# MoBA's position bias from a skewed table: VectorE adds it while it takes the maxima, in place of flip-matrix products on TensorE

## The chip, the cores and the metric

The kernel runs on one core of one Trainium2 chip. The metric is the device time of one execution in microseconds. Lower is better.

## What is computed

Two transformer programs run one after the other (a macaron block of depth 2 with a time mixer, MoBA attention and cross attention, then a second block of depth 2). The change lies in MoBA attention in the first one. There are 256 positions, 8 heads of 64 columns and one block of 256 keys, so the block-sparse attention comes down to causal attention with a position bias:

```python
q = to_heads(q) * (Dh ** -0.5)
...
bias_own = rel_bias[:, rel_bucket(q_pos[:, None] - own_pos[None, :])]
s_own = jnp.einsum('bhqd,bhkd->bhqk', q_c, k_own).astype(f32) + bias_own.astype(f32)[None]
s_own = jnp.where(own_pos[None, :] <= q_pos[:, None], s_own, -jnp.inf)
...
probs = jax.nn.softmax(logits, axis=-1).astype(v.dtype)
```

The bias depends on the head and on the distance of query and key alone. The mask can be written into it: keys ahead of the query have a bias of -1e30.

## The kernel before

Everything of the first program lives in SBUF; weights stream through a ring of six 1 MB slots. Each engine has its own program, written out by hand, and waits on counting semaphores. `nc.sync` loads the weights: a slot is loaded as soon as TensorE has used the tile in it. ScalarE and VectorE split each weight tile into a high and a low part before TensorE multiplies (`col_high`, `col_low`).

A layer goes: feed-forward 1, mixer projection (13 column tiles), MoBA (`moba(l)` on TensorE), the time mixer's solver and recurrence, keys and values of the cross attention, and so on. MoBA starts when the last projection tile (the values `mv`) is copied out of PSUM, and the solver starts when MoBA's last output is copied out.

**The bias.** After feed-forward 1 of layer 0 TensorE makes one row of 512 biases per head (products with a one-hot matrix of distances), and VectorE copies them to `bias_rows`, 8 partitions that lie inside `mv`. GpSimd stores them (16 KB) in DRAM and reads them back with a step of one element per partition (`modulation_program`, L1187 and L1190): `hank[p, h, t] = row_h[p + t]`. This table is in the reverse order of partitions, and a product with the flip matrix `cst["flip"]` turns it round on TensorE. The table is made once and used in both layers. ScalarE waits for the store to be done before it writes to `mv`.

**MoBA.** A head's scores fill one PSUM bank with two query tiles: queries 128 to 255 against 256 keys, and queries 0 to 127 against 128 keys. Four banks rotate. The engines go over the heads like this:

- TensorE (`moba`): in step h `scores(h)`, then `turn(h - 2)` (three 128x128 transposes of the probabilities, L808), then `out(h - 3)` (products with the values, L817 and L818). `scores(h)` has four products: two with the flip matrix (L793, L795), which put the bias into the bank, and two of queries and keys (L797, L799) that add to it.
- VectorE (`softmax`): `maxima(h)` (two maxima over the bank, L1759, and a negation, L1763), then `weights(h - 1)` (reciprocal of the sums, L1768, and two multiplications, L1771), then for every second head the copy of an output pair (L1781). After head 3 it also has `col_low(l, KV0)`, the low part of the first key-value tile (128x2048, L1572).
- ScalarE (`softmax`): `exponential(h)` from PSUM into `prob` with the sum read out (L1351), then `turned(h - 2)`, which copies the turned block to SBUF (L1361).

`prob` has four buffers, so with the exponential of head h ScalarE waits until head h - 4 was turned. TensorE waits with the scores of head h until ScalarE has read the bank of h - 4. The same helper `softmax` serves the cross attention, without bias.

Of the kernel before, what the change touches and what calls it, by code (L numbers as in the profile page):

```python
# [19 lines left out]
ALU = mybir.AluOpType  # L20
# [4 lines left out]
P = 128  # L25
T = 256
# [77 lines left out]
def constants():  # L104

    i = np.arange(P)
    r, c = i[:, None], i[None, :]
    f = lambda m: m.astype(np.float32)
    j, t = i[:, None] % CH, np.arange(CH)[None, :]
    blocks = {  # L110
        "ident": f(r == c),
        "ones": np.ones((P, P), np.float32),
        "head_ones": f(r // HD == c // HD),
        "flip": f(r + c == P - 1),
        "eye": f(j == t),
        "upper": f(j < t),
        "upper_incl": f(j <= t),
        "upper_sub": f((j < t) & (j // SUB == t // SUB)),
        "lower_sub": f((j > t) & (j // SUB == t // SUB)),
        "lower_off": f((j > t) & (j // SUB != t // SUB)),  # L120
    }

    blocks["carry"] = np.tile(f(np.arange(T) % CH != 0), (P, 1))
    return blocks
# [122 lines left out]
def program(nc, a, out):  # L247

    with ExitStack() as ctx:
# [7 lines left out]
        for name, c in constants().items():  # L257
# [12 lines left out]
        store["v_loaded"] = [Signal(ctx, nc, f"v_loaded{s}") for s in range(RING2)]  # L270
        scratch = {"bias": nc.dram_tensor("bias_scratch", (NH, 2 * T), F32).ap(),
                   "mod": nc.dram_tensor("mod_scratch", (DEPTH, P, 2, MODS * P), F32).ap()}
# [10 lines left out]
def build_first(nc, ctx, a, scratch, store):  # L283
# [4 lines left out]
    def sb(name, shape):  # L288
        return ctx.enter_context(nc.sbuf_tensor(name, shape, F32))
# [10 lines left out]
    with ExitStack() as under:  # L300
# [11 lines left out]
        part("under_mem", [P, KD, T])  # L312
        part("under_hank", [P, NH, T])
        g_low = part("g_low", [P, KD, T])
# [20 lines left out]
    mem_sb = sb("mem_sb", [P, KD, T])  # L335
    hank = sb("hank", [P, NH, T])
    mix_buf = sb("mix_buf", [P, RAW + 4 * T])
# [272 lines left out]
    def tensor_program(pe):  # L610
# [175 lines left out]
        def moba(l):  # L786
            def scores(h):
                pair, hb, bank = h // 2, (h % 2) * HD, ps[SCORE_BANKS[h % 4]]
                if h >= 4:
                    pe.wait_ge(*sm_act.at(l, 2 * (h - 3)))  # L790
                hi = slice(hb, hb + HD)

                mm(bank[:, 0:T], cst["flip"], hank[:, h, :], start=True, stop=False,  # L793
                   skip_group_check=True)
                mm(bank[:, T:T + P], cst["flip"], hank[:, h, P:T], start=False, stop=False,  # L795
                   skip_group_check=True)
                mm(bank[:, 0:T], mq[hi, pair, P:T], mk[hi, pair, :], start=False, stop=False,  # L797
                   skip_group_check=True)
                mm(bank[:, T:T + P], mq[hi, pair, 0:P], mk[hi, pair, 0:P], start=False, stop=True,  # L799
                   skip_group_check=True).then_inc(*sc_done.up())  # L800

# [20 lines left out]
            pe.wait_ge(*mix_evac.at(l, MIX_TILES - 1))  # L822
            if l == 0:
                pe.wait_ge(bias_stored.sem, 32)
            for h in range(NH + 3):
# [332 lines left out]
    def modulation_program(pool):  # L1158
# [19 lines left out]
        for n in range(DEPTH * MOD_CHUNKS):  # L1178
# [6 lines left out]
            if n == FFN_STEPS // 2 - 1:  # L1185
                pool.wait_ge(*mem_placed.at(0, 5))
                pool.dma_start(scratch["bias"], bias_rows).then_inc(bias_stored.sem, 16)  # L1187
                pool.wait_ge(bias_stored.sem, 16)
                src = scratch["bias"]
                pool.dma_start(hank[:, :, :], bass.AP(src.tensor, 0, [[1, P], [2 * T, NH], [1, T]])  # L1190
                               ).then_inc(bias_stored.sem, 16)
# [4 lines left out]
    def scalar_program(act):  # L1196
# [144 lines left out]

        def softmax(l, base, scale, widths, banks):

            def exponential(h):
                e, g, bank = h % 4, base + h, ps[banks[h % 4]]
                act.wait_ge(*sm_max.at(l, 3 * (g + 1)))
                if h >= 4:
                    act.wait_ge(*pt_done.at(l, g - 3))
                at = 0
                for t, w in enumerate(widths):  # L1350
                    go(prob[:, e, at:at + w], bank[:, at:at + w], ACT.Exp, bias=smx[:, e, t:t + 1],  # L1351
                       scale=scale, accum_out=ssum[:, e, t:t + 1]).then_inc(*sm_act.up())
                    at += w
# [42 lines left out]
        for l in range(DEPTH):  # L1396
# [72 lines left out]
            col_high(l, KV0)  # L1469
            exponential, turned = softmax(l, 0, 1.0, (T, P), SCORE_BANKS)  # L1470
            for h in range(NH + 2):
# [59 lines left out]
    def vector_program(dve):  # L1531
# [220 lines left out]

        def softmax(l, base, scale, widths, banks):
            def maxima(h):
                e, g = h % 4, base + h
                dve.wait_ge(*sc_done.at(l, g + 1))
                at = 0
                for t, w in enumerate(widths):
                    v.tensor_reduce(smx[:, e, t:t + 1], ps[banks[e]][:, at:at + w], AX_X, ALU.max  # L1759
                                    ).then_inc(*sm_max.up())  # L1760
                    at += w
# [145 lines left out]
        for l in range(DEPTH):  # L1907
# [61 lines left out]
            step(l, v.memset(state[:, :, :], 0.0), seq_step)  # L1969
            maxima, weights = softmax(l, 0, 1.0, (T, P), SCORE_BANKS)  # L1970
            evac = moba_out(l)
# [1603 lines left out]
```

## Time and profile before

| | us |
|---|---|
| median of 3 runs | 2476.46 |
| lowest and highest | 2475.26, 2477.57 |
| span of the profiled execution | 2475.7 |

The profiled execution's own time is not given apart from these runs; its span lies 0.8 us under their median and inside what they spread over. The page gives the busy time of each engine; the trace gives single instructions, merged where alike follow one another. A merged row has the start of the first, the length of all, and in brackets the idle time before it with what ended it.

### The profile page before, as it was taken

The page shows a single profiled execution, that of the slowest core. Times are in us where ns is not written, and L with a number is a line of the kernel's source. Part 1 is how long each engine was busy: PE and PEld are TensorE (multiplying, and loading weights), DVE is VectorE, ACT ScalarE, POOL GpSimd, SP SyncE. Part 2 cuts the span into 40 slices and gives each one's busy share as a digit, 9 for nine tenths or more (in the row PEclk, how much of TensorE's full clock was granted, in tenths as well). Part 3 has the DMA queues.
Part 4 walks back from the last instruction along what each step waited for, and adds up shares of the span by engine and source line. Part 5 has one row for each costly group of instructions (what it writes and reads, how often), then busy time and mean ns, then how long its engine had stood idle before and what let it go on. Part 6 is the DMA issues. An engine that isn't in the chain of part 4 may idle for free. (4 is left out here: it accounts for less than half of the span.)

```text
span 2475.7 us, 41693 instructions
## 1 busy us (share of the span) xinstructions
PE 2411.7 (97%) x17447; PEld 2055.0 (83%) x17447; DVE 1606.0 (65%) x2242; ACT 1033.3 (42%) x1365; POOL 99.2 (4%) x179
## 2 busy tenths in 40 slices
PE   7999999999999999999999999999999999998999
PEld 7999989999999999899999854464888887647999
DVE  6887756778888887657798632671744442474555
ACT  5445534454554455335454321661422222263333
POOL 2010000001101100000001000000000000000000
PEclk9999999999999999999999999999999999999999
DMA  8776503647777775116467742102532331212452
GB/s 283 251 271 216 168 3 120 205 145 267 252 254 239 272 244 160 46 54 213 162 229 255 272 155 68 52 2 71 167 102 90 98 102 52 81 56 69 162 195 69
DMA packets 270807, 381.97 MB, mean 154 GB/s; under 512 B 9593, under 2 KB 235209, under 8 KB 268994
## 3 DMA queue, kind: packets, MB, share of 16 engines
q1 hardware_dynamic: 251628, 314.47, 38.7%
q0 software_dynamic: 18128, 64.20, 7.2%
q8 instruction: 114, 1.87, 0.3%
q10 hardware_dynamic: 902, 1.15, 0.2%
q14 instruction: 35, 0.29, 0.0%
HBM read 366.13 MB, written 13.65 MB: 153 GB/s over the span
## 5 line engine op out<-in xcount | busy, mean ns | idle before, releaser
L704 PE MATMUL ps<-span 128*128 128x512 f32 x1280 | 453.9, 399 | 2.3 <-issue 1.2
L635 PE MATMUL ps<-span,w_low 128*128 128x256 f32 x1440 | 408.0, 283 | 0.0
L706 PE MATMUL ps<-span,w_low 128*128 128x256 f32 x1280 | 359.5, 281 | 0.0
L633 PE MATMUL ps<-span 128*128 128x256 f32 x1216 | 348.6, 287 | 8.2 <-DVE span L1585 5.2
L1603 DVE TENSOR_TENSOR w_low<-ring,span 128x2048 fp32r<-128x2048 f32 x131 | 299.8, 2288 | 82.3 <-ACT span L1267 82.3
L1267 ACT ACTIVATE span<-ring 128x2048 fp32r<-128x2048 f32 x131 | 250.6, 1915 | 135.5 <-DMA ring<-in_ffn_w_in 112.8
L704 PEld LDWEIGHTS ps<-span 128*128 128x128 f32 x1280 | 240.6, 188 | 60.3 <-issue 1.3
L635 PEld LDWEIGHTS ps<-span,w_low 128*128 128x128 f32 x1440 | 277.0, 192 | 0.0
L634 PE MATMUL ps<-span 128*128 128x256 f32 x864 | 245.3, 284 | 0.0
L633 PEld LDWEIGHTS ps<-span 128*128 128x128 f32 x1216 | 233.8, 192 | 12.4 <-DVE w_low L1603 5.4
L706 PEld LDWEIGHTS ps<-span,w_low 128*128 128x128 f32 x1280 | 241.9, 189 | 0.0
L1624 DVE SCALAR_TENSOR_TENSOR mod_acc<-wmod,cond,mod_acc 128x512 f32<-128x512 f32 x336 | 232.3, 748 | 0.4 <-DMA wmod<-in_w_mod 0.4
L634 PEld LDWEIGHTS ps<-span 128*128 128x128 f32 x864 | 166.5, 193 | 0.2
L1572 DVE TENSOR_TENSOR w_low<-ring,span 128x2048 fp32r<-128x2048 f32 x50 | 114.2, 2291 | 51.1 <-ACT span L1210 50.6
L3229 DVE TENSOR_TENSOR w_low<-ring,w_high 128x2048 fp32r<-128x2048 f32 x32 | 73.3, 2292 | 71.8 <-ACT w_high L2958 71.8
L2931 ACT ACTIVATE w_high<-ring 128x2048 fp32r<-128x2048 f32 x32 | 61.2, 1913 | 126.3 <-PE ps L2611 126.3
L1277 ACT ACTIVATE prob<-ps 128x512 f32<-128x512 f32 x80 | 47.7, 596 | 157.0 <-PE ps L706 156.8
L1166 POOL DMA_DIRECT2D wmod<-in_w_mod x96 | 70.6, 735 | 1028.3 <-DVE mod_acc L1624 806.9
L1210 ACT ACTIVATE span<-ring 128x2048 fp32r<-128x2048 f32 x50 | 94.8, 1908 | 21.9 <-PE ps L635 20.5
L2958 ACT ACTIVATE w_high<-ring 128x2048 fp32r<-128x2048 f32 x32 | 61.2, 1916 | 100.4 <-PE ps L2551 100.4
L2705 PE MATMUL ps<-h_sb,ring 128*128 128x512 f32 (+1 forms) x256 | 96.8, 540 | 4.8 <-ACT h_sb L2919 4.6
L2609 PE MATMUL ps<-act_halves,w_high 128*128 128x512 f32 x256 | 100.6, 393 | 0.0
(487 smaller groups left out, 5337.3 us busy)
## 6 DMA issues: line engine op xcount, KB each, us to landing
ring<-in_ffn_w_in SPq DMA_DIRECT2D x88, 1024.0 KB, 8.9
ring<-in_w_mlp SPq DMA_DIRECT2D x64, 1024.0 KB, 5.3
wmod<-in_w_mod POOLq DMA_DIRECT2D x96, 512.0 KB, 6.8
ring<-in_ffn_w_out SPq DMA_DIRECT2D x44, 1024.0 KB, 5.2
ring<-in_w_mix_in SPq DMA_DIRECT2D x26, 1024.0 KB, 5.5
ring<-in_xattn_w_kv SPq DMA_DIRECT2D x16, 1024.0 KB, 5.4
mod_scratch<-mod_acc POOLq DMA_DIRECT2D x24, 512.0 KB, 6.2
ring<-mod_scratch SPq DMA_DIRECT2D x12, 1024.0 KB, 4.9
```

The source lines that it names most:

```text
L633: mm(dst, w_hi, x_hi, start=start, stop=False, **more)
L634: mm(dst, w_hi, x_lo, start=False, stop=False, **more)
L635: return mm(dst, w_lo, x_hi, start=False, stop=stop, **more)
L704: mm(ps[bank + m].rearrange("p (w t) -> p w t", w=2), hi[:, k, cols], span[:, :, k, :], start=(k == 0), stop=False, skip_group_check=True)
L706: last = mm(ps[bank + m][:, 0:T], lo[:, k, cols], h_high[:, k, :], start=False, stop=(k == KD - 1), skip_group_check=True)
L1210: go(w_high[COLUMN_HIGHS[c]], slot(n), ACT.Copy).then_inc(*column_high.up())
L1267: go(w_high[buffer], ring[:, tiles.slot(r, b), :], ACT.Copy).then_inc(w_high_ready.sem, 1)
L1572: v.tensor_tensor(w_low[:, n % RING, :], slot(n), w_high[COLUMN_HIGHS[c]], ALU.subtract).then_inc(*column_low.up())
L1603: v.tensor_tensor(w_low[:, slot, :], ring[:, slot, :], w_high[buffer], ALU.subtract).then_inc(w_low_ready.sem, 1)
L1624: v.scalar_tensor_tensor(mod_acc[:, c, :], w, col, mod_acc[:, c, :], ALU.mult, ALU.add).then_inc(mod_step.sem, 1)
L2609: mm(out, w_hi, x_hi, start=start, stop=False)
L2705: last = mm(ps[bank + m][:, c], wt[:, k, m * P:(m + 1) * P], h[:, k, c], start=(k == 0), stop=(k == KD - 1))
```

## The change

The row of biases is stored 128 times per head (2 MB), once for each partition, and read back with a step of one element less than a row, so that each partition gets the row shifted by one more: `toep[p, h, t] = row_h[127 - p + t]`. This is the table in its right order, so the flip matrix goes. VectorE adds it: in `maxima(h)` one `tensor_tensor_reduce` per query tile reads scores from PSUM and the table from SBUF, writes the sum to `prob` and the maximum to `smx`. The exponentials then read and write `prob`. The wait for the turn of head h - 4 moves from ScalarE to VectorE; TensorE waits with scores(h) for the maxima of h - 4 in place of its exponentials; and the wait for the table in layer 0 moves from TensorE to VectorE.

```diff
-        "flip": f(r + c == P - 1),
...
-        scratch = {"bias": nc.dram_tensor("bias_scratch", (NH, 2 * T), F32).ap(),
+        scratch = {"bias": nc.dram_tensor("bias_scratch", (NH, P, 2 * T), F32).ap(),
...
-    hank = sb("hank", [P, NH, T])
+    toep = sb("toep", [P, NH, T])
...
                 if h >= 4:
-                    pe.wait_ge(*sm_act.at(l, 2 * (h - 3)))
+                    pe.wait_ge(*sm_max.at(l, 3 * (h - 4) + 2))
                 hi = slice(hb, hb + HD)
-
-                mm(bank[:, 0:T], cst["flip"], hank[:, h, :], start=True, stop=False,
-                   skip_group_check=True)
-                mm(bank[:, T:T + P], cst["flip"], hank[:, h, P:T], start=False, stop=False,
-                   skip_group_check=True)
-                mm(bank[:, 0:T], mq[hi, pair, P:T], mk[hi, pair, :], start=False, stop=False,
-                   skip_group_check=True)
-                mm(bank[:, T:T + P], mq[hi, pair, 0:P], mk[hi, pair, 0:P], start=False, stop=True,
-                   skip_group_check=True).then_inc(*sc_done.up())
+                mm(bank[:, 0:T], mq[hi, pair, P:T], mk[hi, pair, :], start=True, stop=True)
+                mm(bank[:, T:T + P], mq[hi, pair, 0:P], mk[hi, pair, 0:P], start=True, stop=True
+                   ).then_inc(*sc_done.up())
...
-            if l == 0:
-                pe.wait_ge(bias_stored.sem, 32)
...
-                pool.dma_start(scratch["bias"], bias_rows).then_inc(bias_stored.sem, 16)
+                pool.dma_start(scratch["bias"], bias_rows.rearrange("h (o t) -> h o t", o=1).to_broadcast(
+                    [NH, P, 2 * T])).then_inc(bias_stored.sem, 16)
...
-                pool.dma_start(hank[:, :, :], bass.AP(src.tensor, 0, [[1, P], [2 * T, NH], [1, T]])
+                pool.dma_start(toep[:, :, :], bass.AP(src.tensor, P - 1, [[2 * T - 1, P], [P * 2 * T, NH], [1, T]])
...
-                e, g, bank = h % 4, base + h, ps[banks[h % 4]]
+                e, g = h % 4, base + h
+                bank = prob[:, e, :] if biased else ps[banks[h % 4]]
                 act.wait_ge(*sm_max.at(l, 3 * (g + 1)))
-                if h >= 4:
-                    act.wait_ge(*pt_done.at(l, g - 3))
...
                 dve.wait_ge(*sc_done.at(l, g + 1))
+                if biases and h >= 4:
+                    dve.wait_ge(*pt_done.at(l, g - 3))
                 at = 0
                 for t, w in enumerate(widths):
-                    v.tensor_reduce(smx[:, e, t:t + 1], ps[banks[e]][:, at:at + w], AX_X, ALU.max
-                                    ).then_inc(*sm_max.up())
+                    if biases:
+                        v.tensor_tensor_reduce(prob[:, e, at:at + w], ps[banks[e]][:, at:at + w], biases(h, t), 1.0,
+                                               -3.0e38, ALU.add, ALU.max, smx[:, e, t:t + 1]).then_inc(*sm_max.up())
+                    else:
+                        v.tensor_reduce(smx[:, e, t:t + 1], ps[banks[e]][:, at:at + w], AX_X, ALU.max
+                                        ).then_inc(*sm_max.up())
...
-            maxima, weights = softmax(l, 0, 1.0, (T, P), SCORE_BANKS)
+            if l == 0:
+                dve.wait_ge(bias_stored.sem, 32)
+            maxima, weights = softmax(l, 0, 1.0, (T, P), SCORE_BANKS, lambda h, t: toep[:, h, t * P:T])
```

TensorE's list in MoBA, one steady step, before (`sm_act` counts exponentials, `sm_norm` weights, `pt_ready` copies of turned blocks):

```order
L793 MATMUL ps<-hank,consts_sb 128x256 [waits sm_act]
L795 MATMUL ps<-hank,consts_sb 128x128
L797 MATMUL ps<-mk,mq 128x256
L799 MATMUL ps<-mk,mq 128x128
L808 MATMUL ps<-consts_sb,prob 128x128 [waits pt_ready,sm_norm]
L808 MATMUL ps<-consts_sb,prob 128x128 x2
L817 MATMUL ps<-probT,mv 64x256 [waits pt_ready]
L818 MATMUL ps<-probT,mv 64x128
```

The same step now (`sm_max` counts maxima):

```order
L791 MATMUL ps<-mk,mq 128x256 [waits sm_max]
L792 MATMUL ps<-mk,mq 128x128
L801 MATMUL ps<-consts_sb,prob 128x128 [waits pt_ready,sm_norm]
L801 MATMUL ps<-consts_sb,prob 128x128 x2
L810 MATMUL ps<-probT,mv 64x256 [waits pt_ready]
L811 MATMUL ps<-probT,mv 64x128
```

The two bias products are gone, and the wait of the step stands at the scores.

VectorE's list in MoBA, the step of head 5, before (`sc_done` counts scores, `av_out` output copies):

```order
L1759 TENSOR_REDUCE smx<-ps 128x1 [waits sc_done,av_out]
L1759 TENSOR_REDUCE smx<-ps 128x1
L1763 TENSOR_SCALAR smx<-smx 128x2 [waits sm_max]
L1768 RECIPROCAL ssum<-ssum 128x2 [waits sm_act]
L1771 TENSOR_SCALAR prob<-prob,ssum 128x256 [waits sm_norm]
L1771 TENSOR_SCALAR prob<-prob,ssum 128x128
```

The same step now (`pt_done` counts turns):

```order
L1753 ISA prob,smx<-ps,toep 128x256 [waits pt_done,sc_done,av_out]
L1753 ISA smx 128x1
L1753 ISA prob,smx<-ps,toep 128x128
L1753 ISA smx 128x1
L1760 TENSOR_SCALAR smx<-smx 128x2 [waits sm_max]
L1765 RECIPROCAL ssum<-ssum 128x2 [waits sm_act]
L1768 TENSOR_SCALAR prob<-prob,ssum 128x256 [waits sm_norm]
L1768 TENSOR_SCALAR prob<-prob,ssum 128x128
```

Each maximum became an addition with a running maximum and a separate readout of it (the rows with `smx` alone), and the wait for the turn stands at the head of the step.

## Rows read from the trace of the kernel before

**Rows 1.** The page, its span and part 1: busy time of each engine.
```profile
span 2475.7 us, 41693 instructions
...
PE 2411.7 (97%) x17447; PEld 2055.0 (83%) x17447; DVE 1606.0 (65%) x2242; ACT 1033.3 (42%) x1365; POOL 99.2 (4%) x179
```

**Rows 2.** Windows, MoBA in both layers: length, busy per engine, granted clock, DMA share, GB/s.
```profile
302.98:327.75 24.77, 23.60 (x121) 16.95 (x121) 14.97 (x53) 12.25 (x41) 0.00 (x0) 1.00 0.13 43
1001.31:1026.08 24.77, 23.60 (x120) 16.95 (x121) 14.98 (x53) 12.21 (x41) 0.00 (x0) 1.00 0.14 43
```

**Rows 3.** Timeline, TensorE, one steady head: start, us, engine, line, operation [idle before].
```profile
317.24 0.70 PE L793 MATMUL ps<-hank,consts_sb 128*128 128x256 f32 x2
...
318.09 0.70 PE L797 MATMUL ps<-mk,mq 64*128 64x256 f32 x2
...
318.93 0.55 PE L808 MATMUL ps<-consts_sb,prob 128*128 128x128 f32 x3
...
319.41 0.65 PE L817 MATMUL ps<-probT,mv 128*64 128x256 f32 x2
...
320.20 0.70 PE L793 MATMUL ps<-hank,consts_sb 128*128 128x256 f32 x2
```

**Rows 4.** Timeline, all engines, the first head of layer 0.
```profile
303.80 0.70 PE L797 MATMUL ps<-mk,mq 64*128 64x256 f32 x2
...
304.83 0.62 DVE L1759 TENSOR_REDUCE smx<-ps 128x1 f32<-128x256 f32 x2 [4.26 <-PE ps L799]
...
305.48 0.17 DVE L1763 TENSOR_SCALAR smx<-smx 128x2 f32<-128x2 f32 x1
...
305.69 0.47 ACT L1351 ACTIVATE prob<-ps,smx 128x256 f32<-128x256 f32 x1 [1.00 <-DVE smx L1763]
...
306.06 0.19 ACT L1351 ACTIVATION_READ_ACCUMULATOR prob<-ps,smx 128x1 f32 x1
306.15 0.36 ACT L1351 ACTIVATE prob<-ps,smx 128x128 f32<-128x128 f32 x1
...
306.40 0.20 ACT L1351 ACTIVATION_READ_ACCUMULATOR prob<-ps,smx 128x1 f32 x1
...
307.19 0.16 DVE L1768 RECIPROCAL ssum<-ssum 128x2 f32<-128x2 f32 x1
...
307.38 0.55 DVE L1771 TENSOR_SCALAR prob<-prob,ssum 128x256 f32<-128x256 f32 x2
```

**Rows 5.** Groups by form, whole span: busy us, mean ns of one, idle before.
```profile
L1572 DVE TENSOR_TENSOR w_low<-ring,span 128x2048 fp32r<-128x2048 f32 x50 | 114.2, 2291 | 51.1 <-ACT span L1210 50.6
...
L1759 DVE TENSOR_REDUCE smx<-ps 128x1 f32<-128x256 f32 x32 | 12.8, 422 | 23.3 <-PE ps L799 18.1 <-PE ps L1028 5.2
...
L1814 DVE TENSOR_TENSOR sc<-ps,sc 128x256 f32<-128x256 f32 x24 | 10.2, 425 | 17.7 <-PE ps L873 17.5
...
L1361 ACT ACTIVATE probT<-ps 128x384 f32<-128x384 f32 x16 | 7.7, 489 | 2.0 <-PE ps L808 2.0
```

**Rows 6.** Groups by form: VectorE's multiply-add of two SBUF tensors and a scalar column.
```profile
L1624 DVE SCALAR_TENSOR_TENSOR mod_acc<-wmod,cond,mod_acc 128x512 f32<-128x512 f32 x336 | 232.3, 748 | 0.4 <-DMA wmod<-in_w_mod 0.4
```

**Rows 7.** Groups by form: a ScalarE pass of 128x512 from PSUM and from SBUF.
```profile
L1277 ACT ACTIVATE prob<-ps 128x512 f32<-128x512 f32 x80 | 47.7, 596 | 157.0 <-PE ps L706 156.8
...
L1282 ACT ACTIVATE prob<-prob 128x512 f32<-128x512 f32 x40 | 24.7, 618 | 11.4 <-DVE prob L1636 11.2
```

**Rows 8.** Timeline, layer 0: the first turn and the last output copy.
```profile
308.04 0.55 PE L808 MATMUL ps<-consts_sb,prob 128*128 128x128 f32 x3
...
327.18 0.42 DVE L1781 COPY cat<-ps 128x256 f32<-128x256 f32 x1 [1.57 <-PE ps L818]
```

**Rows 9.** GpSimd's store, the read of the table (DMA view), ScalarE's first write to `mv`.
```profile
217.74 0.55 POOL L1187 DMA_DIRECT2D bias_scratch<-mv  x1 [21.39 <-DVE mv L1924]
...
hank<-bias_scratch POOLq DMA_DIRECT2D x1, 1024.0 KB, 6.0
...
294.84 0.60 ACT L1334 ACTIVATE mv<-ps 128x512 f32<-128x512 f32 x1 [3.41 <-PE ps L764]
```

More of the change, by code:

```diff
@@ L312, in build_first @@
         part("under_mem", [P, KD, T])
-        part("under_hank", [P, NH, T])
+        part("under_toep", [P, NH, T])
         g_low = part("g_low", [P, KD, T])
@@ L1340, in cross_part, with softmax @@
                ).then_inc(*cross_high.up())
-        def softmax(l, base, scale, widths, banks):
+        def softmax(l, base, scale, widths, banks, biased=False):
             def exponential(h):
-                e, g, bank = h % 4, base + h, ps[banks[h % 4]]
+                e, g = h % 4, base + h
+                bank = prob[:, e, :] if biased else ps[banks[h % 4]]
                 act.wait_ge(*sm_max.at(l, 3 * (g + 1)))
-                if h >= 4:
-                    act.wait_ge(*pt_done.at(l, g - 3))
                 at = 0
@@ L1469, in scalar_program @@
             col_high(l, KV0)
-            exponential, turned = softmax(l, 0, 1.0, (T, P), SCORE_BANKS)
+            exponential, turned = softmax(l, 0, 1.0, (T, P), SCORE_BANKS, True)
             for h in range(NH + 2):
@@ L1751, in shift, with softmax @@
                                                b[:, m, 1:T + 1], ALU.mult, ALU.add), mixed)
-        def softmax(l, base, scale, widths, banks):
+        def softmax(l, base, scale, widths, banks, biases=None):
             def maxima(h):
```

## The prediction

> **What bounds the kernel now.** I read the page first: TensorE is busy 97% of a span of 2475.7 us, VectorE 65%, ScalarE 42% [rows 1]. So time is won only where TensorE's own list gets shorter and nothing else steps in. The change touches one stage that runs once per layer, MoBA's attention, so next I read the windows of that stage: 24.77 us in each of two layers, with TensorE busy for 23.60 of it, VectorE for 14.97, ScalarE for 12.2, at a granted clock of 1.00 [rows 2]. The timeline of one head in the steady part shows TensorE going round without a gap: bias products and scores from 317.24, of which the bias products last to 318.09 (0.85 us), the scores to 318.93 (0.84), the turning of probabilities to 319.41 (0.48), the products with the values to 320.20 (0.79) [rows 3]. A head costs 2.97 us, and VectorE and ScalarE idle inside it. That is the limit that the change attacks, 0.85 of each 2.97 us.
>
> **What goes from TensorE.** Two products per head, 0.85 us, 8 heads, 2 layers: 13.6 us of TensorE's time. This would be the gain only if the others kept up, and 2.12 us per head is about what their chain needs, so I worked that chain out.
>
> **The prices on the other engines.** From the first head of layer 0 [rows 4]: the maximum sees a finished score product 0.18 us after its end (303.80 + 0.85, then 304.83); the two maxima take 0.62, the negation follows 0.03 later and takes 0.17; ScalarE's exponentials start 0.04 after it and end at 306.60, 0.91 later. The weights (reciprocal and two multiplications) take from 307.19 to 307.93. ScalarE's copy of the turned block takes 0.49, the copy of an output pair on VectorE 0.42 [rows 5, 8]. Between such steps 0.03 to 0.06 us pass, 0.10 to 0.15 after a product. The large subtraction for the first key-value tile that sits in VectorE's list after head 3 takes 2.29 [rows 5].
>
> **What VectorE gets.** In place of two maxima it issues four instructions per head: an addition with running maximum over 256 columns, a readout of the maximum, the same for 128 columns, another readout. Call the length of this block M; before it is 0.62. No such instruction is in the trace. The main part is nearest to the addition of a PSUM and an SBUF tensor of 128x256, 425 ns, which equals the maximum's 422 ns [rows 5], so the main parts alone leave M at 0.62. For the readout the nearest row is ScalarE's: 0.19 us long, but the next exponential starts 0.09 after it (306.06, 306.15), because it overlaps the end of its main part [rows 4]. With that overlap M = 0.62 + 0.09 + 0.09 = 0.80. With no overlap at all it is 0.42 + 0.20 + 0.28 + 0.20 = 1.10. Bounds: 0.62 if readouts are hidden; above, 1.5, if the main part also runs at half rate (256 and 128 columns more at the 1.1 ns per column of the 2291 ns subtraction over 2048 [rows 5], 0.42 us). I take M = 0.90, nearer the row with the overlap, with 0.10 for an instruction form that nothing here has timed.
>
> The microarchitecture reference of the Trainium skill (Vector Engine (DVE) Microarchitecture Reference, section "Points that are easy to get wrong") says that an accumulating two-source instruction with both fp32 sources in SBUF runs at half rate. By it alone M would be about 1.3 to 1.5. Here one source is PSUM; and the two-SBUF-source form without accumulation takes 748 ns for 512 columns [rows 6], far from half rate, but no row has the accumulating form.
>
> **What ScalarE gets.** The exponentials read SBUF in place of PSUM. The same 128x512 pass over SBUF took 618 ns, over PSUM 596 [rows 7]: 0.022 more each, 0.05 per head. Its wait for the earlier turn goes (to VectorE, below). Setting this to 0 changes the sum by 0.3 us.
>
> **The waits that move.** VectorE now waits before head h's block, for h of 4 and up, until TensorE has turned head h-4. Queued behind that wait are all its later weights and output copies, and TensorE waits for those; but the turn of h-4 lies two rounds back in TensorE's list, so I cost it at nothing. TensorE's wait before scores(h) is now on the maxima of h-4, also long past: nothing. What replaces them is the plain supply of probabilities.
>
> **The replay.** I went through the 8 heads list by list: an instruction starts at the later of its engine's previous end and its releaser. With the costs of before it puts the last output copy at 327.5 against 327.18 in the trace, a fair check (0.2 of it is one turn that overlaps the next bias product). With the bias products out and M = 0.90:
> - Scores(0) start at 302.98 as before [rows 4], maxima(0) at 304.01 in place of 304.83. VectorE then does maxima(1) at 305.02 and must wait for the exponentials of head 0: weights(0) at 306.14, turn(0) at 306.94. Before it was at 308.04 [rows 8]. TensorE has been idle 1.4 us, so of 2.55 us taken from its list 1.10 is gained.
> - Turn(1) 308.64; turn(2) 311.00. VectorE's 2.2 us subtraction lies from 310.23 to 312.43. Maxima(4) follow it, weights(3) at 313.44, turn(3) at 314.24, after a wait of 1.1 (before, TensorE did not notice the subtraction).
> - After that a round of two heads is closed through ScalarE: scores and their 0.18 (1.03), block and negation (0.90 + 0.24), exponentials (0.85), copy (0.54), values (0.79) = 4.35, or 2.18 per head, against 2.12 that TensorE needs. The turns come at 316.60, 318.72, 320.71 and 322.22.
> - The last output copy starts at 324.43, 3.1 us before the replay of the old kernel; in the trace it starts at 327.18 and the next stage at 327.75 [rows 2, 8].
>
> So 3.1 us per layer, 6.2 in all, less than half of the 13.6. The sum by other M, from the same replay, both layers: 0.62 gives 8.6 less; 0.80, 7.2; 1.00, 5.0; 1.10, 3.6; 1.20, 2.2; 1.36, nothing; 1.50, 2.1 more; 1.70, 5.3 more. What follows the stage waits for its last copy on TensorE, so the gain is passed on; the weight loads there are released by TensorE's use, and move with it.
>
> **The table.** The row of biases is now written to DRAM 128 times, 2 MB in place of 16 KB, once, from 217.74, and read back skewed. The 1 MB read took 6.0 us [rows 9], so 2 MB are 12, and I allow twice that because it leaves from few partitions. So it lands by 242, and the table by 250. ScalarE needs the row's place at 294.84 [rows 9], VectorE the table at 304. So I cost it at nothing: ScalarE's own work covers it with 50 us to spare, and past that it costs the delay itself. The weight loads that share the DMA engines with it are issued six tiles ahead.
>
> **Sum.** The profiled span is 2475.7, the median of the three runs 2476.46 (0.8 above; the fastest is 2475.26). 2476.46 - 6.2 = 2470.3 us.
>
> **Rivals.** What a measurement here can tell from no change is about 0.2%, 5 us.
> - *Readouts do not overlap* (M 1.0 to 1.3). For: a readout needs the last column's result; against: ScalarE's overlaps. 2471.5 to 2475.9, at M = 1.1 2472.9. 0.27.
> - *Readouts are hidden* (M to 0.75): 2468, for: VectorE's small instructions overlap by 0.08 each. 0.06.
> - *The block runs at half rate*, as the skill's rule above would have it if PSUM does not help: M = 1.5, VectorE becomes the bound, 2478.6. Against it, the 748 ns. 0.10.
> - *Slower:* this kind of instruction has a fixed cost of its own that nothing hides, since every one waits for or feeds the next. Place: VectorE's block between score and exponential. Four per head; from M = 1.36 (0.14 each above the 0.80 sum) the kernel loses, from 1.68 (0.22 each) by over 5 us; at M = 1.7, 2481.8. For: no instruction of this form has a row. Against: all others on VectorE keep to one line of length over columns. 0.06.
> - *The table is late*, because 128 copies leave from only 8 partitions: it would need over three times the 24 us. 2480 or far more. 0.02.
> - *The change does not do what it says*, as the gain is taken back by a later wait: within 2 us of 2476.5. 0.03.
>
> **Numbers.** The forecast (M 0.75 to 1.0, 2468.9 to 2471.5) has 0.46. Faster by over 0.2% is this and the hidden readouts, less a little at the edge: 0.50. Within 0.2%: 0.27 + 0.10 + 0.03 + that edge = 0.42. Slower: 0.08. The range goes from 2467.8 (M = 0.62) to 2478.0, which leaves out the two slow cases and half of the half-rate one.
>
> **What would show it.** In the stage's window: TensorE's turns 2.1 to 2.2 us apart in place of 2.97, now with idle time released by VectorE's weights or ScalarE's copy; turn(0) at 1.1 us earlier; stage 21.7 us long in both layers. The new instructions near 425 and 280 ns and readouts that add 0.1. I am wrong if the main part is over 0.5 us, if the readouts stand beside it in full, if turn(3) comes later than 315, or if ScalarE's conversion near 294.8 waits for the stored row.

## The result and the profile after

| | time, median us | runs | profiled span |
|---|---|---|---|
| before | 2477.02 | 4 (2475.26 to 2479.95) | 2475.7 |
| changed | 2499.02 | 4 (2498.95 to 2500.17) | 2496.9 |

The changed kernel is slower: its ratio to the kernel before is 1.0093, with a 95% interval of 1.0079 to 1.0108. I had forecast 2470.3. That is 22 us in the runs and 21.2 us in the profiled span, and the span can be taken apart.

The page of the changed kernel: its span, the busy time of each engine, and the granted clock over 40 slices.

```profile
span 2496.9 us, 41593 instructions
...
PE 2418.5 (97%) x17383; PEld 2055.2 (82%) x17383; DVE 1606.6 (64%) x2274; ACT 1033.5 (41%) x1365; POOL 99.5 (4%) x179
...
PEclk9999989999999999899999999999999999999999
```

Against [rows 1], TensorE executes 64 instructions fewer and is busy for 6.8 us *longer* (2418.5 against 2411.7). An engine with less work and more busy time points to its clock. The slices of 62 us are too coarse to show where. The windows below are finer: MoBA's stage in both layers, then pieces of the stage in layer 0, then two stretches ahead of it. Columns as in [rows 2].

```profile
316.31:344.39 28.08, 25.16 (x88) 15.90 (x89) 15.33 (x69) 12.65 (x41) 0.00 (x0) 0.64 0.12 38
1018.71:1046.79 28.08, 25.17 (x88) 15.63 (x89) 15.33 (x69) 12.57 (x41) 0.00 (x0) 0.64 0.12 38
316.31:320.10 3.79, 1.55 (x13) 1.30 (x13) 2.30 (x14) 3.49 (x9) 0.00 (x0) 1.00 0.85 262
322.00:341.00 19.00, 19.00 (x55) 11.58 (x56) 10.90 (x46) 7.33 (x27) 0.00 (x0) 0.50 0.00 1
341.00:344.39 3.39, 2.71 (x15) 1.64 (x14) 0.85 (x2) 0.64 (x2) 0.00 (x0) 0.95 0.00 0
262.00:266.00 4.00, 0.00 (x0) 0.00 (x0) 0.00 (x0) 1.50 (x1) 1.02 (x2) 0.61 0.94 307
266.00:270.00 4.00, 1.04 (x5) 1.07 (x6) 3.41 (x4) 3.51 (x5) 0.00 (x0) 0.50 1.03 338
```

Two things are to be seen. The stage takes 28.08 us in place of 24.77, in both layers, and for most of it the granted clock is 0.50, the level of 1.2 GHz, where [rows 2] show 1.00, that of 2.4 GHz. And the stage of layer 0 begins at 316.31 in place of 302.98: 13.3 us were lost before it, and from 262 to 266 TensorE does nothing at all. So 13.3 + 3.3 + 3.3 = 19.9 of the 21.2 us have a place. The other 1.3 lie in the rest of the program, which the change does not touch; nothing here shows what they are.

**The first place.** The DMA view of 215 to 275 us (what is written, from what, queue, count, size, median us from issue to landing), then the time to landing of the loads that were issued from 215 to 270:

```profile
ring<-in_w_mix_in SPq DMA_DIRECT2D x6, 1024.0 KB, 26.2
bias_scratch<-mv POOLq DMA_DIRECT2D x1, 2048.0 KB, 45.0
toep<-bias_scratch POOLq DMA_DIRECT2D x1, 1024.0 KB, 9.3
...
DMA to landing us min/median/max: 13.7/26.2/41.1
```

The timelines of SyncE (an issue of a load), ScalarE and TensorE, with the idle time before an instruction in brackets:

```profile
223.40 0.37 SPq L551 DMA_DIRECT2D ring<-in_w_mix_in  x1
...
264.50 1.91 ACT L1202 ACTIVATE span<-ring 128x2048 fp32r<-128x2048 f32 x1 [15.23 <-DMA ring<-in_w_mix_in]
...
268.96 0.55 PE L632 MATMUL ps<-span 128*128 128x256 f32 x1 [10.06 <-DVE w_low L1563]
```

The store of the table takes 45.0 us, from 218.16 to 263.2; the one of 16 KB before took 1.8. The median of 26.2 us for the 1 MB loads of mixer weights mixes two kinds. The three that were issued while the store ran, at 223.40, 229.99 and 236.90, took 41.1, 37.4 and 36.4 us, and the first of them landed only at 264.5, behind the end of the store. In the kernel before, the loads issued at 222.97, 229.55 and 236.47 took 7.3, 5.3 and 5.3. The issue at 236.90 also took 24.55 us itself in place of 0.37, so the loads behind it left late. GpSimd's own wait for the store (44.2 us) costs nothing. The wait that does is ScalarE's for the load of 223.40: ScalarE comes for it at 249.27, 25.9 us after its issue, and waits 15.23. The wait passes through VectorE's `w_low` to TensorE, which stands idle for 10.06. Inside that idle time the granted clock falls to 0.50, and it is back at 1.00 in the window of 274 to 276. So 10.1 of the 13.3 us are idle time, and of the 3.3 behind it the slow clock is a part. The table itself came in time: it landed near 273, and ScalarE, which needs the row's place in `mv`, came to it only at 308.13.

**The second place.** The timeline of the changed kernel, TensorE and VectorE, start of the stage and two later steps (start, us, [idle before]):

```profile
316.31 0.71 PE L791 MATMUL ps<-mk,mq 64*128 64x256 f32 x4 [0.78 <-ACT mv L1326]
...
317.04 0.59 PE L791 MATMUL ps<-mk,mq 64*128 64x256 f32 x2
...
317.39 0.42 DVE L1753 CUSTOM_DVE_ANT_0 prob<-ps,toep 128x256 f32<-128x256 f32 x1 [3.52 <-PE ps L792]
...
317.74 0.08 DVE L1753 DVE_READ_ACCUMULATOR2_ANT smx<- 128x1 f32 x1
317.74 0.28 DVE L1753 CUSTOM_DVE_ANT_0 prob<-ps,toep 128x128 f32<-128x128 f32 x1
317.95 0.08 DVE L1753 DVE_READ_ACCUMULATOR2_ANT smx<- 128x1 f32 x1
318.07 0.17 DVE L1760 TENSOR_SCALAR smx<-smx 128x2 f32<-128x2 f32 x1
...
320.10 0.55 PE L801 MATMUL ps<-consts_sb,prob 128*128 128x128 f32 x3 [2.24 <-DVE prob L1768]
...
324.19 1.22 PE L791 MATMUL ps<-mk,mq 64*128 64x256 f32 x2
...
328.07 1.22 PE L791 MATMUL ps<-mk,mq 64*128 64x256 f32 x2
```

The scores of heads 0 to 2 are done at 317.86. Then TensorE waits 2.24 us for the first probabilities. The granted clock is 1.00 up to 320 and 0.50 from 321 on. From then on the same score product takes 1.22 us in place of 0.70 [rows 3], and one head takes 3.88 us (324.19 to 328.07).

VectorE's new block runs from 317.39 to 318.03, so the prediction's M, the length of this block, is 0.64. The main parts take 0.42 and 0.28. The first readout (0.08) begins at the same time as the second main part, the last one ends the block.

So two theories stand for the 22 us. The **store theory**: the store of 2 MB costs 12 to 13 us, through the weights. The **clock theory**: TensorE's idle time ahead of `turn(0)` (the first turn, which waits for the first probabilities) drops its clock, and that costs the stage more than the change takes from it. The main rival of the second: VectorE is the bound of the shorter stage (a block too long, a wait moved wrong), and the clock follows from a TensorE that waits.

### The profile page after: what moved, and what is told of

Same layout as the page of the kernel before. It is cut to its first block and busy times, and to the rows that moved or that the text cites. A ratio compares the mean times of both kernels' runs of the same rounds, so it can differ in the third digit from the quotient of the medians.

```text
span 2496.9 us, 41593 instructions
## 1 busy us (share of the span) xinstructions
PE 2418.5 (97%) x17383; PEld 2055.2 (82%) x17383; DVE 1606.6 (64%) x2274; ACT 1033.5 (41%) x1365; POOL 99.5 (4%) x179
## 5 line engine op out<-in xcount | busy, mean ns | idle before, releaser
L632 PEld LDWEIGHTS ps<-span 128*128 128x128 f32 x1216 | 234.8, 193 | 22.3 <-issue 12.4
```

Source lines behind the costliest of these rows:

```text
L632: mm(dst, w_hi, x_hi, start=start, stop=False, **more)
```

## Experiments

**1. The table is made without the wide store.** The row goes to DRAM once, is copied there 128-fold from DRAM to DRAM, and then read as in the change.

```
-        scratch = {"bias": nc.dram_tensor("bias_scratch", (NH, P, 2 * T), F32).ap(),
+        scratch = {"row": nc.dram_tensor("bias_row", (NH, 2 * T), F32).ap(),
+                   "bias": nc.dram_tensor("bias_scratch", (NH, P, 2 * T), F32).ap(),
...
-                pool.dma_start(scratch["bias"], bias_rows.rearrange("h (o t) -> h o t", o=1).to_broadcast(
+                pool.dma_start(scratch["row"], bias_rows).then_inc(bias_stored.sem, 16)
+                pool.wait_ge(bias_stored.sem, 16)
+                pool.dma_start(scratch["bias"], scratch["row"].rearrange("h (o t) -> h o t", o=1).to_broadcast(
                     [NH, P, 2 * T])).then_inc(bias_stored.sem, 16)
-                pool.wait_ge(bias_stored.sem, 16)
+                pool.wait_ge(bias_stored.sem, 32)
...
-                dve.wait_ge(bias_stored.sem, 32)
+                dve.wait_ge(bias_stored.sem, 48)
```

> The change, but the 2 MB of shifted biases are made otherwise: the 16 KB of rows are stored once from SBUF, a DRAM to DRAM transfer copies them 128 times, and the table is read back as before. Theory: the store that leaves from 8 partitions held the DMA engines for 45 us and starved the mixer weights, 13.3 us ahead of MoBA in layer 0; from DRAM the 2 MB take under 15 us, the stall goes, MoBA starts near 303 us, and the time is 2499.0 - 13.3 = 2485 to 2486 us, with the granted clock still near 0.64 over MoBA in both layers. Rival: 2 MB more of traffic at that place is the trouble however they are made; then most of the stall stays and the time is above 2493.

Measured: 2486.83 us in the median of 6 runs; ratio to before 1.0039 (1.0026 to 1.0051), 12 us less than the changed kernel (12.4 by the profiled spans, 2484.5 against 2496.9). Its DMA view of the same stretch, and its windows of the stage:

```profile
ring<-in_w_mix_in SPq DMA_DIRECT2D x7, 1024.0 KB, 5.5
bias_scratch<-bias_row POOLq DMA_DIRECT2D x1, 2048.0 KB, 16.1
```

```profile
303.16:331.31 28.15, 25.23 (x88) 15.82 (x89) 15.32 (x69) 12.64 (x41) 0.00 (x0) 0.64 0.13 38
1006.45:1034.55 28.10, 25.21 (x89) 15.85 (x89) 15.32 (x69) 12.64 (x41) 0.00 (x0) 0.64 0.13 38
```

The same 2 MB take 16.1 us. The loads of weights take 5.5 in the median; the three issued at 223 to 237, during the copy or just behind it, take 14.1, 10.4 and 9.3, which is slower than before but inside the 25.9 us that ScalarE leaves them. ScalarE has no wait for weights, and the stage begins at 303.16, close to the 302.98 of before. It is still 28.1 us long at a clock of 0.64. The two losses are apart.

**2. The wide store alone, in the kernel before.** Everything stays as it was, flip products too, but the row is stored 128 times, and `hank` is read from the first copy of each head.

```
-        scratch = {"bias": nc.dram_tensor("bias_scratch", (NH, 2 * T), F32).ap(),
+        scratch = {"bias": nc.dram_tensor("bias_scratch", (NH, P, 2 * T), F32).ap(),
...
-                pool.dma_start(scratch["bias"], bias_rows).then_inc(bias_stored.sem, 16)
+                pool.dma_start(scratch["bias"], bias_rows.rearrange("h (o t) -> h o t", o=1).to_broadcast(
+                    [NH, P, 2 * T])).then_inc(bias_stored.sem, 16)
...
-                pool.dma_start(hank[:, :, :], bass.AP(src.tensor, 0, [[1, P], [2 * T, NH], [1, T]])
+                pool.dma_start(hank[:, :, :], bass.AP(src.tensor, 0, [[1, P], [P * 2 * T, NH], [1, T]])
```

> The kernel before with the 128-fold store from 8 partitions alone; the table is still read in the old order and the flip products stay. Theory: the store alone gives the 13.3 us ahead of MoBA in layer 0, so 2477.0 + 13.3 = 2490 us, MoBA itself stays at 24.77 us and clock 1.00 in both layers. Rival (the stall comes from the new order of waits, not from the store): 2477 us.

Measured: 2490.6 us (5 runs), ratio 1.0053 (1.0036 to 1.0069). DMA view and window:

```profile
ring<-in_w_mix_in SPq DMA_DIRECT2D x6, 1024.0 KB, 25.7
bias_scratch<-mv POOLq DMA_DIRECT2D x1, 2048.0 KB, 44.8
```

```profile
316.01:340.77 24.76, 23.59 (x120) 16.94 (x121) 14.97 (x53) 12.24 (x41) 0.00 (x0) 1.00 0.15 43
```

The store costs 12.1 us in a kernel that has nothing else of the change (2490.6 against 2478.49, the kernel before beside it), and leaves the stage at 24.76 us and full clock. The three loads issued during the store took 40.9, 37.2 and 36.5 us, and ScalarE waited 15.0 for the first, as in the changed kernel. The store theory is shown from both sides.

**3. The idle time is filled.** On experiment 1, four products into the eighth PSUM bank stand before `turn(0)`. They add work, and nothing reads their result.

```
                 if h < NH:
                     scores(h)
+                if h == 2:
+                    for _ in range(4):
+                        mm(ps[7][:, 0:T], ident, mk[:, 0, :], start=True, stop=True)
                 if 2 <= h < NH + 2:
                     turn(h - 2)
```

> The copy made from DRAM, and four idle-time products of 128x256 (identity by keys, into a bank that nobody reads) on TensorE between the scores of head 2 and the turn of head 0, where it now idles 2.24 us. Theory (the clock falls because TensorE idles there): clock 1.00 through MoBA in both layers, the stage is 20.5 to 22 us in place of 28.08, and the time is 2485.5 - 2 x 6.5 = 2471 to 2473 us or below. Rival (the clock falls because the whole stage has less work per us without the flip products): the clock still falls to 0.50 a little later, and the time stays at 2484 to 2487.

Measured: 2470.21 us (10 runs), ratio 0.9967 (0.9956 to 0.9977), faster than both kernels. Windows of the stage, and TensorE's timeline:

```profile
303.45:324.29 20.84, 18.22 (x96) 12.31 (x97) 15.05 (x69) 12.55 (x41) 0.00 (x0) 1.00 0.17 51
999.47:1020.28 20.81, 18.23 (x97) 12.31 (x97) 15.05 (x69) 12.55 (x41) 0.00 (x0) 1.00 0.16 52
```

```profile
304.93 1.99 PE L822 MATMUL ps<-mk,consts_sb 128*128 128x256 f32 x8
307.23 0.55 PE L802 MATMUL ps<-consts_sb,prob 128*128 128x128 f32 x3 [0.31 <-DVE prob L1774]
...
313.83 0.55 PE L802 MATMUL ps<-consts_sb,prob 128*128 128x128 f32 x3 [0.62 <-DVE prob L1774]
...
315.36 0.70 PE L792 MATMUL ps<-mk,mq 64*128 64x256 f32 x2
...
317.48 0.70 PE L792 MATMUL ps<-mk,mq 64*128 64x256 f32 x2
```

The 1.99 us of products are the whole edit. `turn(0)` starts 3.78 us after the first scores, as in the changed kernel (3.79), so nothing came earlier. But the clock stays at 1.00, and the stage takes 20.8 us in place of 28.1. A head takes 2.12 us (315.36 to 317.48). The rival falls: with VectorE's list untouched, the stage shrinks by 7.3 us. VectorE as a bound does show once, in the 0.62 us before `turn(3)` (313.83), behind its long subtraction.

**4. The idle time alone, in the kernel before.** `turn(0)` also waits for the weights of head 1. No product is taken out and no instruction added.

```
-                pe.wait_ge(*sm_norm.at(l, 3 * (h + 1)))
+                pe.wait_ge(*sm_norm.at(l, 3 * (h + 1 if h else 2)))
```

> The kernel before, flip products and all; the turn of head 0 waits in addition for the weights of head 1, so TensorE idles some 1.6 us there. Theory (an idle of this size at this place is enough for the clock): the clock falls to 0.50 within MoBA, each layer's stage is 30 to 36 us, the time 2490 to 2499. Rival (the density of the stage decides): clock 1.00, 1.6 us more per layer, 2480. It could also be that 1.6 us are too short where 2.24 are not; then the rival's numbers appear without the rival being right.

Measured: 2485.59 us (6 runs), ratio 1.0036 (1.0022 to 1.005), less than I expected. Timeline and windows:

```profile
309.88 0.90 PE L808 MATMUL ps<-consts_sb,prob 128*128 128x128 f32 x3 [1.56 <-DVE prob L1771]
```

```profile
303.18:332.74 29.56, 26.82 (x120) 19.01 (x121) 15.05 (x53) 12.35 (x41) 0.00 (x0) 0.88 0.12 36
...
310.00:316.00 6.00, 6.00 (x19) 4.13 (x19) 2.25 (x7) 1.91 (x8) 0.00 (x0) 0.50 0.00 0
318.00:332.74 14.74, 13.57 (x71) 9.16 (x71) 7.85 (x31) 6.12 (x22) 0.00 (x0) 1.00 0.00 0
```

Idle time of 1.56 us was enough here to halve the clock in a stage of which nothing else was changed; layer 1 had 1.57 us and lost its clock too. The stage of layer 0 takes 29.56 us, of which the later turn explains 1.6 (309.88 - 303.18 = 6.70 against 5.06 before, [rows 4, 8]), and the clock the other 3.2. What I had wrong is how long it lasts. Here TensorE is back at 1.00 after 7 us, in the changed kernel after 21.

**5 and 6. How much idle time it takes.** As experiment 3, with one product (`range(1)`) and with two (`range(2)`).

> As fill4 with one product; about 1.7 us of idle time are left, as in before_idle, where the clock fell. Theory: the clock falls in both layers and the time is 2480 to 2487. Rival: as fill2.

> As fill4, with two of the idle-time products in place of four, so about 1.2 us of idle time are left before the turn of head 0. Theory (the length of the idle time at the start of the stage decides): either the clock holds and the time is that of fill4, 2468 to 2472, or it falls and the time is 2478 to 2486; nothing in between within one layer. Rival (the amount of work put in matters, not the gap): between the two, near 2476.

Measured: one product 2482.68 us (10 runs, spread from 2474.4 to 2487.0), ratio 1.0015 (0.9999 to 1.003), which is not to be told from no change; two products 2472.01 (10 runs), ratio 0.998 (0.9964 to 0.9996). With one product, `turn(0)` of layer 0 and of layer 1, then both windows:

```profile
306.69 0.55 PE L802 MATMUL ps<-consts_sb,prob 128*128 128x128 f32 x3 [1.61 <-DVE prob L1774]
...
1001.63 0.55 PE L802 MATMUL ps<-consts_sb,prob 128*128 128x128 f32 x3 [1.57 <-DVE prob L1774]
```

```profile
302.91:323.75 20.84, 16.93 (x91) 11.17 (x91) 15.05 (x69) 12.55 (x41) 0.00 (x0) 1.00 0.16 51
997.89:1025.92 28.03, 25.79 (x90) 16.09 (x91) 15.34 (x69) 12.65 (x41) 0.00 (x0) 0.63 0.12 38
```

With two products, layer 0:

```profile
306.53 0.55 PE L802 MATMUL ps<-consts_sb,prob 128*128 128x128 f32 x3 [1.18 <-DVE prob L1774]
```

The same kernel, with the same 1.6 us of idle time, keeps its clock in one layer and loses it in the other, and it is the layer with the slightly longer idle time that keeps it. At 1.18 us both layers of the profiled run kept it (stages of 20.84 and 20.79), and at 2.24 both lost it. The other runs have only a mean clock over the whole execution. With four products it is 0.992 to 0.997, with one product 0.986 to 0.992, and the profiled run that lost one layer has 0.990. With two products eight runs have 0.994 to 0.997, but the other two, the longest at 2479.14 and 2481.00 us, have 0.989. That fits one layer lost in each of these two, so 1.18 us is probably not safe either; no trace was kept of them. For the same idle time both outcomes occur, and nothing here shows what decides. The Trainium skill (TensorE: Matmul & The Clock Gate, "Part 1: The HAM clock gate (the "warmup" mystery)") says that the unit that sets the clock runs free of the program, so that one kernel changes level at different points in different runs. The two layers of this profiled run differ in the same way.

**7 and 8. What keeps the clock down.** The changed stage asks less of TensorE per head than the one before, and the fall lasted three times as long. So on experiment 1 two products like the old bias products stand ahead of each head's scores, which overwrite them: in 7 from head 3 on, so that the idle time stays; in 8 for all heads (the condition is then `if True:`), so that it goes. Their result is not used.

```
+                if h >= 3:
+                    mm(bank[:, 0:T], ident, mem_sb[:, 0, :], start=True, stop=True)
+                    mm(bank[:, T:T + P], ident, mem_sb[:, 0, P:T], start=True, stop=True)
                 mm(bank[:, 0:T], mq[hi, pair, P:T], mk[hi, pair, :], start=True, stop=True)
```

> As dram_copy (2.2 us idle before the turn of head 0), but from head 3 on the scores are preceded by two products of the size of the flip products whose result is overwritten. Theory (idle time starts the fall, and what follows decides how long it lasts): the clock falls to 0.50 but comes back after about 7 us as in before_idle, not 20, stage 28 to 31 us, time 2483 to 2490. Rival (the fall lasts 20 us whatever follows): 0.50 for 20 us with the longer list, stage 33 us or more, time above 2492.

> As dram_copy, with two overwritten products of the size of the flip products ahead of the scores of every head: TensorE's list is as long as before the change, VectorE does its new work. Theory (VectorE's new block is hidden behind TensorE's 2.97 us per head): clock 1.00, stage within 0.5 us of 24.77 us, time 2476 to 2480, as before. Rival (the new block or the moved wait costs time by itself): stage over 25.5 us and time above 2480.

Measured: from head 3 on, 2489.18 us (5 runs), ratio 1.0051 (1.0035 to 1.0066); for all heads, 2478.59 (10 runs), 1.0006 (0.9995 to 1.0017). Windows, first of experiment 7, then of 8:

```profile
303.44:330.19 26.75, 23.23 (x109) 16.26 (x109) 15.15 (x69) 12.54 (x41) 0.00 (x0) 0.87 0.13 40
1003.92:1033.45 29.53, 26.04 (x109) 17.92 (x109) 15.23 (x69) 12.56 (x41) 0.00 (x0) 0.77 0.11 36
```

```profile
303.25:328.16 24.91, 23.60 (x120) 16.98 (x121) 15.14 (x69) 12.69 (x41) 0.00 (x0) 1.00 0.14 43
```

With the longer list after the fall, the clock is 0.87 in one layer and 0.77 in the other, in place of 0.64 in both: the fall lasted about 7 and 14 us. So the longer list went with a shorter fall, but not with one value, and I can't say from these runs what decides between 7 and 14. Experiment 8 is plainer: it has all of VectorE's and ScalarE's side of the change, all of TensorE's old load and no idle time ahead of `turn(0)`, and its stage takes 24.91 us at full clock, 0.14 more than before. VectorE's new block and the moved waits cost next to nothing.

**9 and 10. Do the two costs add up, and does experiment 3 repeat?** Experiment 9 is the changed kernel, wide store and all, with the four products of experiment 3; experiment 10 is experiment 3 again.

> The changed kernel as it is, store from 8 partitions and all, with the four idle-time products of fill4. Theory (store and clock are two separate costs that add up): the 13.3 us ahead of MoBA in layer 0 stay, clock 1.00 through MoBA in both layers, so 2470.2 + 13.3 = 2483 to 2485 us. Rival (the stall also sets the clock in MoBA): the clock falls in MoBA of layer 0 although the gap is filled, 2487 to 2492.

> fill4 once more, as the measure for the kernel beside it: 2466 to 2474 us.

Measured: 2482.12 us (10 runs), ratio 1.0022 (1.0012 to 1.0032), and 2472.38 (8 runs), 0.9975 (0.9962 to 0.9988). Window of experiment 9:

```profile
315.58:336.42 20.84, 18.22 (x96) 12.30 (x97) 15.05 (x69) 12.54 (x41) 0.00 (x0) 1.00 0.16 51
```

The stage starts late by the store and is short by the full clock. The products take 16.9 us off the changed kernel (2499.02 to 2482.12), and 16.6 or 14.5 off the one with the DRAM copy (2486.83 to 2470.21 or 2472.38). The store costs 12.2 us without them and some 10 to 12 with them. The two are independent within the measurement.

**11. More overlap.** The score products of an even and an odd head use different halves of the rows. In [rows 3] one head's take 0.84 us; in the changed kernel's timeline two heads' take 0.73 together (316.31 to 317.04) where they are neighbours. So on experiment 3 the order puts them next to each other wherever it can.

```
-            for h in range(NH + 3):
-                if h < NH:
-                    scores(h)
...
+            ahead = "s0 s1 s2 s3 f t0 s4 s5 t1 o0 t2 o1 s6 s7 t3 o2 t4 o3 t5 o4 t6 o5 t7 o6 o7".split()
+            for name in ahead:
+                if name == "f":
+                    for _ in range(4):
+                        mm(ps[7][:, 0:T], ident, mk[:, 0, :], start=True, stop=True)
+                else:
+                    dict(s=scores, t=turn, o=out)[name[0]](int(name[1]))
```

> fill4 with the scores of two heads always next to each other on TensorE, since the first two of the changed kernel took 0.73 us together where one alone takes 0.85. Theory (pairs overlap everywhere, and TensorE's list gets 0.5 us shorter per head for heads 2 to 7, so that VectorE's 1.7 us per head bounds): stage 19 to 20 us in place of 20.8, clock 1.00, 2 to 4 us less than fill4. Rival (VectorE and ScalarE already bound the stage): the same as fill4, or, if new idle times drop the clock, 5 us and more above it.

Measured: 2469.84 us (7 runs), ratio 0.9967 (0.9955 to 0.9979). Window:

```profile
303.30:323.22 19.92, 16.10 (x97) 10.54 (x97) 14.96 (x69) 12.54 (x41) 0.00 (x0) 1.00 0.18 54
```

TensorE's work falls from 18.22 to 16.10 us, but the stage only from 20.84 to 19.92, since TensorE now waits more for the others. Some 0.9 us per layer is below what the runs resolve: the time is not to be told from experiment 10's, 2472.38, beside it. Both beat the kernel before.

## Why the prediction was wrong

The direction was wrong, and with it the range. By the steps of the prediction:

- **"Two products per head", gone from TensorE: right.** The claim that less than half of the 13.6 us comes back was too low: at full clock the stages gain 3.93 and 3.96 us (24.77 to 20.84 and 20.81), 7.9 in all, which is 58%.
- **M, taken at 0.90: too high; 0.64 measured**, near the lower bound of 0.62 that the addition's 425 ns [rows 5] gave. The error was to price the readouts by ScalarE's row and to add 0.10 for an unknown form. The same replay gives about 8.5 us less for 0.64, and experiment 3 has 7.9 in its stages. The forecast's own mechanism, VectorE's block between score and exponential, held at full clock; the rival *readouts are hidden*, at 0.06, was the one that came true. *Half rate*, by the Trainium skill's rule (Vector Engine (DVE) Microarchitecture Reference, "Points that are easy to get wrong"), did not: the 256 columns take 0.42 us, with one source in PSUM. No run here had both in SBUF.
- **ScalarE's exponentials from SBUF, +0.05 per head: right in size.** In the timeline they take 0.51 and 0.39, before 0.47 and 0.36.
- **The moved waits, costed at nothing: right.** Experiment 8 holds them all and its stage takes 0.14 us more than before.
- **The table, "So I cost it at nothing": the first step that failed, by 12 to 13 us.** Its size was wrong: I allowed 24 us for the store and it took 45.0. That alone would have been harmless, as the table had 50 us to spare. What I missed is whom the store holds up. I wrote that the weight loads "are issued six tiles ahead" and left it there. In time the lead was 25.9 us for the load that ScalarE waited for (223.40 to 249.27). That is ample for a load of 5 to 7 us and too little for one of 41.1, and the difference is the 15.2 us that ScalarE stood at `ring`. My rival *the table is late* watched ScalarE's write to `mv` and VectorE's wait for the table, and neither waited for it. The question to ask was what else moves by DMA meanwhile, and at what pace it must be served.
- **The replay's "TensorE has been idle 1.4 us": the second step that failed, by some 15 us.** I booked this idle time ahead of `turn(0)` at its own length and at nothing for what comes behind it. It was 2.24: I gave three heads' scores 2.5 us, but with no bias product between them neighbours overlap, and they take 1.55. Even 1.4 us lies between the 1.18 at which the profiled run kept its clock and the 1.56 at which one lost it. The stage was forecast at 21.7 us, would be 20.8 at full clock, and is 28.1 with the clock at 0.50 for 21 us of it. I had read the granted clock of 1.00 in [rows 2] as a property of the stage. In these runs it went with TensorE's unbroken list, which the change was about to break. None of my rivals had a clock in it. Both costs lie outside every mechanism to which I gave a chance, which is how 0.08 for slower came about.

The sum as it came out, in the profiled spans: 7.9 us less for TensorE's shorter list, 14.5 more in the two stages for the clock (28.1 against 20.8 us), 13.3 more ahead of the stage for the store (12.1 in the times of experiment 2), and 1.3 in the rest of the span, together 21.2.

## What to carry to other kernels

When an edit takes work from an engine that never pauses, look for the pause it opens, above all at the start of a pipeline, and ask for the granted clock behind it. If nothing useful can be moved there, a few products whose result nobody reads can keep the clock: here 2 us of them in each layer won 14 to 17 us in all. And a large transfer that is "long done before it is needed" is not free by that: before calling it hidden, name the loads that are issued while it runs and who waits for them. Compare the slowest of them, not the median, with the time between its issue and its use. Where the source is a few partitions, try the copy inside DRAM.

## What the runs showed of the hardware

- Idle time of TensorE of 2.2 us, inside a stage that is otherwise full, halved its clock (1.00 to 0.50 in the records) in both layers; 1.56 and 1.57 us did so in the kernel before; about 1.6 us did in one layer and not in the other; 1.18 us did not in a profiled run, but two other runs of that kernel have the low mean clock (0.989) of a lost layer. The clock fell behind the idle time (in the changed kernel it is 1.00 up to 320 and 0.50 from 321, with work since 320.10) or inside it (in layer 1 of experiment 7 it fell at 1007.0, with TensorE idle from 1005.5 to 1007.66; in the changed kernel's wait for weights between 262 and 264). In the stage it stayed down for about 7, 14 or 21 us. The shorter list behind the fall (heads of 2.12 us at full clock) went with 21, the longer one (2.97) with 7 or 14. What sets the length stays open.
- A store of 2 MB from 8 partitions took 45 us and held the DMA share at 0.50 for most of that time, as this window of the changed kernel shows:

```profile
250.00:254.00 4.00, 4.00 (x29) 3.79 (x29) 2.22 (x3) 0.00 (x0) 0.00 (x0) 1.00 0.51 64
```

  The 1 MB loads issued while it ran took 36 to 41 us in place of 5 to 7. From DRAM to DRAM the same bytes took 16.1 us, and loads issued during it or just behind it 9 to 14. For the share of one half the Trainium skill has a reason (DMA: Bandwidth & Descriptors, "Why a DMA increments its semaphore by 16 and not by 1"): a transfer is split over as many engines as divide the slowest dimension of both its sides, at most 16, which is 8 here. That fits the 0.50. It does not explain why the copy inside DRAM, whose slowest dimension is 8 too, was almost three times as fast; that a read of few partitions is slow in itself is my guess, and no run tested it.
- VectorE's addition with a running maximum takes 0.42 and 0.28 us for 256 and 128 columns. The plain maximum takes 422 ns for 256 [rows 5] and 281 for 128. The readout of 0.08 us starts before the main part ends, and the whole block takes 0.64 us in place of 0.62.
- Score products of 64 rows on opposite halves overlap when they are neighbours in TensorE's list: two heads in 0.73 us, against 0.84 for one. With all of them next to each other TensorE's busy time in the stage fell from 18.22 to 16.10 us.
